# Second layer's mixture of experts: fixed slots for the first two pairs, 2 MB weight loads in the loop, and rearranged scatters and tail work

## What is computed

```python
MOE_GROUPS, MOE_EXPERTS_PER_GROUP, MOE_TOP_K, MOE_HIDDEN = 4, 8, 2, 512     # 32 experts
# router: one group of the four, then two of its eight experts; weights sum to the group's probability
# for every token: sum over its two experts of
#     weight * (silu(x @ w_gate[e]) * (x @ w_up[e])) @ w_down[e]
# w_gate, w_up: (32, 1024, 512)   w_down: (32, 512, 1024)
# then  h + expert sum, and a final rms_norm with gain final_norm_g
```

## Time and profile before

| | |
|---|---|
| median of 3 runs | 998.7 us (997.88 to 1004.07) |
| the profiled execution: span from the first to the last instruction | 997.7 us |
| bytes read from HBM | 338.07 MB |
| TensorE busy, weight loads of TensorE busy | 92%, 49% |
| VectorE, ScalarE, GpSimd busy | 30%, 21%, 2% |
| mean granted TensorE clock | 0.992 |

### The profile page before, as it was taken

The page is one execution under the profiler, slowest core; times in us unless marked ns, Lnnn a source line. Parts: engine busy times, 40 slices in busy tenths (PEclk is TensorE's granted clock), DMA queues, the critical chain, the costliest instruction groups (busy, mean ns, idle before and its releaser), DMA issues.

```text
span 997.7 us, 11975 instructions
## 1 busy us (share of the span) xinstructions
PE 915.7 (92%) x4621; PEld 486.7 (49%) x4621; DVE 304.2 (30%) x658; ACT 207.9 (21%) x440; POOL 22.9 (2%) x60
## 2 busy tenths in 40 slices
PE   8998999999999998999999999988887788887996
PEld 5776566555655555866447333333333233333332
DVE  3345357333332334132126132222201122201113
ACT  3232353112111114024324111111101111101112
POOL 4001300000000000000000000000000000000000
PEclk9999999999999998999999999999999999999999
DMA  9940455999999999644228999999999999999994
GB/s 312 388 174 1 168 191 206 422 420 422 419 421 421 419 421 388 247 143 168 85 82 349 423 415 422 420 421 421 422 422 422 421 423 421 422 422 421 422 422 191
DMA packets 62607, 339.77 MB, mean 341 GB/s; under 512 B 10877, under 2 KB 11921, under 8 KB 25570
## 3 DMA queue, kind: packets, MB, share of 16 engines
q1 hardware_dynamic: 56690, 337.60, 83.8%
q10 hardware_dynamic: 5456, 1.39, 0.7%
q0 software_dynamic: 416, 0.16, 0.2%
HBM read 338.07 MB, written 1.05 MB: 340 GB/s over the span
## 4 chain that ended last, share of the span: by engine, by line
PE 63%; DMA 28%; DVE 5%; ACT 2%; issue 1%; SPq 0%; DVEq 0%; ACTq 0%
DMA ring<-in_expert_w_up_dram 23%; PE ps L1005 22%; PE ps L1069 9%; PE ps L2070 7%; PE ps L2218 5%; PE ps L2283 4%; PE ps L1088 4%; DMA ring<-in_expert_w_down_dram 2%; DMA ring<-in_w_up_dram 2%; PE ps L2058 1%; PE ps L967 1%; PE ps L1195 1%; PE ps L1382 1%; PE ps L2193 1%; PE ps L1017 1%
## 5 line engine op out<-in xcount | busy, mean ns | idle before, releaser
L1005 PE MATMUL ps<-ring,work 128*64 128x256 f32 (+1 forms) x2048 | 344.3, 489 | 48.0 <-DMA ring<-in_expert_w_up_dram 23.9
L1005 PEld LDWEIGHTS ps<-ring,work 128*64 128x64 f32 x2048 | 151.6, 137 | 242.0 <-issue 207.1
L1069 PE MATMUL ps<-ring,work 128*64 128x512 f32 x688 | 156.1, 598 | 1.1 <-DMA ring<-in_expert_w_down_dram 0.9
L823 DVE TENSOR_TENSOR work<-work,ps 128x256 f32<-128x256 f32 (+1 forms) x30 | 16.4, 546 | 275.8 <-PE ps L1005 275.8
L1069 PEld LDWEIGHTS ps<-ring,work 128*64 128x64 f32 x688 | 47.9, 136 | 88.7 <-issue 88.2
L2070 PE MATMUL ps<-xT,ring 128*128 128x256 f32 (+1 forms) x384 | 86.3, 383 | 0.0
L2070 PEld LDWEIGHTS ps<-xT,ring 128*128 128x128 f32 x384 | 72.5, 191 | 11.4 <-issue 1.2
L1088 PE MATMUL ps<-parts 128*128 128x512 f32 x248 | 73.5, 419 | 2.2 <-DVE parts L844 2.2
L676 ACT ACTIVATE work<-ps,small 128x512 f32<-128x512 f32 x30 | 20.6, 688 | 196.6 <-PE ps L1069 196.6
L670 ACT ACTIVATE work<-ps 128x256 f32<-128x256 f32 (+1 forms) x31 | 15.1, 489 | 212.4 <-PE ps L1043 212.4
L2218 PE MATMUL ps<-ring,work 128*128 128x512 f32 x128 | 56.0, 595 | 2.2 <-ACT work L1708 1.8
(11 more groups left out here) (380 smaller groups left out, 676.3 us busy)
## 6 DMA issues: line engine op xcount, KB each, us to landing
ring<-in_expert_w_gate_dram SPq DMA_DIRECT2D x64, 1024.0 KB, 23.4
ring<-in_expert_w_up_dram SPq DMA_DIRECT2D x64, 1024.0 KB, 23.6
ring<-in_expert_w_down_dram SPq DMA_DIRECT2D x58, 1024.0 KB, 22.8
ring<-in_w_gate_dram SPq DMA_DIRECT2D x32, 1024.0 KB, 16.8
ring<-in_w_up_dram SPq DMA_DIRECT2D x32, 1024.0 KB, 18.3
ring<-in_w_down_dram SPq DMA_DIRECT2D x32, 1024.0 KB, 15.9
ring<-in_w_in_dram SPq DMA_DIRECT2D x18, 1024.0 KB, 15.6
ring<-in_w_out_dram SPq DMA_DIRECT2D x8, 1024.0 KB, 11.4
```

The costliest lines, as they stand in the source:

```text
L823: dve.tensor_tensor(hs[:, 0:ff], sil[:, 0:ff], ps[:, 5, 0:ff], ALU.mult).then_inc(ev(f"h{sfx}"), 1)
L1005: mm = pe.matmul(ps[CAP * e:CAP * e + CAP, 4 + which, 0:ff], slots, chunks[e][:, k, :], start=(k0 + k == 0), stop=(k0 + k == KC - 1), skip ...
L1069: mm = pe.matmul(ps[CAP * e:CAP * e + CAP, 6 + half, :], hT[:, c0 + k, CAP * e:CAP * e + CAP], columns(chunks[e], k, half), start=(c0 + k ...
```

## The change

- **Fixed slots.** Experts 0 to 3 (pairs 0 and 1) get 64 fixed slots each. Their one-hot rows (`fixed`) need only each token's place within its expert, not the packed order. `gather_fixed` forms them with 32 matmuls of 256 columns; VectorE and ScalarE (`take_fixed`) copy the result straight to `xg2`, each feature block when it is done, and the gates of pair 0 start block by block. The packed gather is still made, for pairs 2 to 15: its 32 matmuls of 512 columns stand in `opening` in two parts (`gather_rest`), and `onehot` is written behind the fixed copies.
- **Order and asides.** `OPENING` streams gates and ups of pairs 0 and 1 first, then both downs. The 6 chunks beside the ring are others: one of pair 0's gates, one of its downs, all 4 of pair 2's downs. Five of their loads stand ahead of place 8 in SP's order (`load_aside_early`), the rest ahead of place 12. GpSimd copies a row of numbers for the one-hot rows, so that its old place can take weights.
- **2 MB loads.** For pairs 4 to 13 (the loop) one load brings a whole matrix of one expert into two neighbouring slots (`load_whole`), 16 KB in a row in each partition. It waits until both slots are free: 3 or 4 chunks of a group of four used. TensorE waits for both experts' matrices at once.
- **Spread scatters.** In the loop (`spaced_pair`) the first half of pair n-1's scatter stands ahead of pair n's gates, the second between gates and ups.
- **Tail.** The gain row is loaded by ScalarE's queue and spread in pair 12, the residual rows are added in pair 13, both between gates and ups; pairs 12 and 13 are written out for that. Some loads of the tail wait for one more used chunk.

```diff
+def whole_weights(gate, up, down, ff, pair):
+    out = []
+    for w, c, n in ((gate, KC, ff), (up, KC, ff), (down, ff // P, D)):
+        v = w[0].rearrange("e (p c) n -> e p c n", c=c)
+        for e in range(2):
+            out.append((v[bass.ds(2 * pair + e, 1), :, :, :].rearrange("e p c n -> p (e c) n"), (c, n)))
+    return out
...
-        ASIDE = {"m1": (0, 0, 0), "m2": (4, 0, 2)}
...
+        ASIDE = {"m1": {}, "m2": {(0, 3): "aside3", (0, 11): "aside_pieces1", (2, 8): "aside0", (2, 9): "aside2",
+                                  (2, 10): "aside1", (2, 11): "aside_pieces0"}}
...
+        OPENING = ([(0, j) for j in range(8)] + [(1, j) for j in range(8)] + [(0, j) for j in range(8, 12)]
+                   + [(1, j) for j in range(8, 12)])
...
+        def two_slots(slot, shape):
+            return ring[:, slot:slot + 2, :].rearrange("p s n -> p (s n)").rearrange("p (a b) -> p a b", b=shape[1])
+        WHOLE = {"m1": PAIRS, "m2": 4}
+        WHOLE_LAPS = LAST_A - WHOLE["m2"]
...
+            def load_whole(n0, spec, turn, per_turn, freed):
+                src, shape = spec
+                sp.wait_ge(chunk_used, turn * per_turn + (n0 - RING + freed))
+                sp.dma_start(two_slots(n0 % RING, shape), src).then_inc(landed[n0 % RING], 16)
...
+            def load_aside_early(cfg):
+                sp.wait_ge(ev("rs_ready"), 8)
+                load_whole_aside(cfg, "aside0")
                 for k in range(2):
                     for half in range(2):
...
+                        load_piece(cfg, "aside_pieces0", k, half)
+                sp.wait_ge(*nth("vdp", 2))
+                load_whole_aside(cfg, "aside2")
+                load_piece(cfg, "aside_pieces1", 1, 0)
+                sp.wait_ge(*nth("numbers", 1))
+                load_piece(cfg, "aside_pieces1", 0, 0)
+                sp.wait_ge(ev("mTp"), 4)
+                load_piece(cfg, "aside_pieces1", 1, 1)
+                load_whole_aside(cfg, "aside3")
+            def load_aside_late(cfg):
+                sp.wait_ge(ev("router_pe"), 3)
+                load_whole_aside(cfg, "aside1")
+                sp.wait_ge(ev("routed"), 2)
+                load_piece(cfg, "aside_pieces1", 0, 1)
...
+                            if tag == "m2" and place == cfg["base"] + RING - 4:
+                                load_aside_early(cfg)
+                            if tag == "m2" and place == cfg["base"] + RING:
+                                load_aside_late(cfg)
...
+                            if p0 >= WHOLE[tag]:
+                                wholes = whole_weights(cfg["gate"], cfg["up"], cfg["down"], cfg["ff"], i * 2 + (p0 + k))
+                                for w, spec in enumerate(wholes):
+                                    load_whole(place_in_stream(cfg, p0 + k, 2 * w), spec, i, 2 * cfg["per"], 3 - w % 2)
+                                continue
...
+                        if j < RING and j % 4 == 1:
+                            sp.wait_ge(chunk_used, cfg["tail"] + j - RING + 2)
                         load(cfg["tail"] + j, spec, 0, 0)
-                        if j == 0:
-                            sp.dma_start(gain_row[0:1, :], t["final_norm_g_2"].rearrange("(a n) -> a n", a=1))\
-                                .then_inc(ev("gain_row"), 16)
...
+            pool.wait_ge(ev("odp"), TT)
+            pool.tensor_copy(numbers, from_one[:, :]).then_inc(ev("numbers"), 1)
...
+            def take_fixed(f):
+                act.wait_ge(*nth("fixed_pe", f // 2 + 1))
+                act.activation(xg2[:, :, f, :], ps[:, f // 2, 256 * (f % 2):256 * (f % 2) + 256]
+                               .rearrange("p (b s) -> p b s", b=2), ACT.Copy, scale=gk[:, cfg["gains"], f:f + 1])\
+                    .then_inc(ev("fixed_scalar"), 1)
...
-                bring(1, 1, ev("xg"))
                 take_gates(0)
+                take_gathered(1)
                 take_turned_hidden(n)
-                bring(2, 0, ev("xg"))
+                take_gathered(3)
                 take_gates(1)
+                take_gathered(5)
+                take_gathered(7)
                 take_down(0)
                 take_turned_hidden(n + 1)
+                act.wait_ge(ev("placed"), 5 * TURN[tag])
+                act.wait_ge(ev("xgP_even"), 4 * TURN[tag])
+                act.wait_ge(ev("xgP_odd"), 4 * TURN[tag])
+                bring(2, 0, ev("xg"))
...
                 build_weighted(0, n)
                 hidden(n, 0)
+                take_gathered(0)
+                take_gathered(2)
+                hidden(n + 1, 1)
+                take_gathered(4)
+                take_gathered(6)
                 take_scatter(n)
                 build_weighted(1, n + 1)
...
+            def gather_fixed():
+                def slots_of(f, tt, v, first, last):
+                    return pe.matmul(ps[:, f // 2, 256 * (f % 2):256 * (f % 2) + 256], v[:, tt, f, :].bitcast(F32R),
+                                     fixed[:, tt, :].bitcast(F32R), start=first, stop=last, skip_group_check=True)
+                for tt in range(TT):
+                    pe.wait_ge(ev("xs_high"), TT * turn_ + tt + 1)
+                    pe.wait_ge(*nth("fixed", tt + 1))
+                    for f in range(KC):
+                        slots_of(f, tt, xs_high, tt == 0 and f % 2 == 0, False)
+                for tt in range(TT):
+                    pe.wait_ge(ev("xs_low"), TT * turn_ + tt + 1)
+                    for f in range(KC):
+                        mm = slots_of(f, tt, xs_low, False, tt == 1)
+                        if tt and f % 2:
+                            mm.then_inc(ev("fixed_pe"), 1)
+            def gather_rest(groups):
+                pe.wait_ge(ev("onehot"), TT * TURN[tag])
+                for f in groups:
+                    if f >= 4:
+                        pe.wait_ge(ev("xgP_odd" if f % 2 else "xgP_even"), 4 * turn_ + (f - 4) // 2 + 1)
+                    else:
+                        pe.wait_ge(*nth("fixed_scalar" if f % 2 else "fixed_vector", KC // 2))
+                    for tt in range(TT):
+                        part(f, tt, xs_high, tt == 0, False)
+                        mm = part(f, tt, xs_low, False, tt == 1)
+                    mm.then_inc(ev("gathered"), 1)
...
+                    if pair >= WHOLE[tag]:
+                        for e in range(2):
+                            first = place_in_stream(cfg, pair, j - j % 4 + 2 * e)
+                            if j % 4 == 0:
+                                pe.wait_ge(landed[first % RING], turn * (16 * (2 * per // RING)) + 16 * (first // RING + 1))
+                            views.append(chunk_view(first % RING + j % 4 // 2, shape))
+                        return views
...
-                j = gates_and_ups(getter(0, 0), chunk_used, n, 0, True)
+                j = gates_and_ups(getter(0, 0), chunk_used, n, 0, pair=0)
+                gather_rest((0, 1))
                 turn_hidden(n)
+                gather_rest((2, 3))
+                gates_and_ups(getter(1, 0), chunk_used, n + 1, 1, pair=1)
+                gather_rest((4, 6, 5, 7))
                 turn_weights(n)
-                gates_and_ups(getter(1, 0), chunk_used, n + 1, 1)
                 down(getter(0, 0), chunk_used, j, n, pair=0)
+                pe.wait_ge(ev("xgP_even"), 4 * TURN[tag])
                 scatter(n, 0, True, False)
                 turn_hidden(n + 1)
+                pe.wait_ge(ev("xgP_odd"), 4 * TURN[tag])
...
+            def spaced_pair(pair, p0, turn, n):
+                scatter(n - 1, 0, False, False)
+                def between():
+                    scatter(n - 1, 1, False, False)
+                    if isinstance(pair, int) and pair == LAST_A - 2:
+                        spread_gain_row()
+                    if isinstance(pair, int) and pair == LAST_A - 1:
+                        for half in range(2):
+                            add_rows(half)
+                j = gates_and_ups(getter(p0, turn), chunk_used, n, p0 % 2, between=between)
+                if isinstance(pair, int) and pair == LAST_A - 2:
+                    pe.wait_ge(*nth("gain_ready", 2))
+                turn_hidden(n)
+                turn_weights(n)
+                down(getter(p0, turn), chunk_used, j, n, pair=p0)
             if tag == "m2":
+                gather_fixed()
                 opening(EARLIER[tag])
+                two_pairs(1, 1, 0, False)
+                turns = (LAST_A - 4) // 2 - 1
+                with pe.Fori(0, turns) as i:
+                    for odd in range(2):
+                        spaced_pair(None, 4 + odd, i, i * 2 + (EARLIER[tag] + 4 + odd))
+                for odd in range(2):
+                    p = 4 + 2 * turns + odd
+                    spaced_pair(p, 4 + odd, turns, EARLIER[tag] + p)
...
+            row = {"m1": from_one[:, :], "m2": numbers}[tag]
+            if tag == "m2":
+                dve.wait_ge(*nth("numbers", 1))
```

(17 more changed lines are left out.)

244 lines of the change are left out of this document (132 added, 112 removed).

## The result

| | before | after |
|---|---|---|
| median of 20 runs each | 999.9 us | 995.8 us |
| lowest, highest | 997.9, 1006.5 | 994.5, 999.7 |
| ratio, 95% interval | | 0.995, 0.9932 to 0.9967 |
| profiled execution, span | 997.7 | 993.7 |
| last load landed on its last engine | 984.34 | 980.34 |

The change is worth 0.5%, 4 to 5 us, less than the 1% that the prediction takes for no change. The span is 4.0 us shorter, and the last load lands 4.0 us earlier; from there to the end it is 13.4 us in both.

What follows compares the result with a forecast made beforehand. From pair 4 on the weights' DMA rate (422 GB/s) was taken as the bound. Span 997.7 less 2.0 (opening) and 4.5 (2 MB loads), nothing for scatters and tail, gave 991.2, so 992.2 us for the median; range 988.5 to 1001.

Steps and rivals of the forecast that it cites:

- the 1% that the prediction takes for no change: Whole kernel: about 1% (10 us) is what a measurement can tell from no change.
- The call, within 1% and a little faster: Whole kernel: 992.2 us forecast; chance 0.80 of within 1%, 0.13 of faster by more, 0.07 of slower.
- The prediction's narrower range, 989 to 995: Whole kernel: the forecast's own range, from 0 to 3.6 us for the opening and 2.2 to 5.1 for the packets.
- Gates at 537.8, SP's place 12 at 541.5: Opening: second layer's first gates start at 537.8 instead of 542.7, 4.9 us earlier; SP issues place 12 at 541.5.
- TensorE spends the head start: Pairs 0 to 3: added TensorE work uses up the 4.9 us and loses 1.4; pair 3 starts at 614.7.
- The pause ahead of the first 2 MB load: Before pair 4: place 42 needs 33 used chunks, not 31, waits until 621.6; a DMA pause of over 3 us.
- The opening's term, 2.0: Opening: places 42 and 43 land at 629.4 instead of 631.5, 2.1 us gained, taken as 2.
- A constant lag of the last engine: Weight stream: the most backward DMA engine sets the time; the pause lets it catch up, later instruction fetches may undo that.
- The rate, 4.5 us: Loop: 16 KB packets cost 1.7% less than two of 8 KB, taken as 1.5% of 298 us, 4.5 us gained.
- Scatters and tail at nothing: Loop and tail: scatters lie under waits, moved gain and residual rows were hidden; gain nothing, bound 0.5 us.
- PEclk at 1.00 in the loop: Loop: sign that the forecast is right, TensorE's granted clock stays at 1.00.
- The slower rival: Loop: three waits a pair lower TensorE's clock, a pair takes 31.5 us, the kernel 1013.7; 5%.

Runs made afterwards that it cites:

- e1_small: The changed kernel with 1 MB loads in the loop instead of 2 MB loads; 997.4 us, ratio 0.9969 to before.
- e4_late_whole: The changed kernel with pairs 4 and 5 loaded in 1 MB chunks and 2 MB loads only from pair 6 on; 996.7 us, ratio 0.9968 to before.
- after_again: The changed kernel measured once more with nothing altered; 996.2 us, ratio 0.9953 to before.
- e2_split: The changed kernel with each 2 MB load of the loop issued as two of 1 MB, same waits; 1000.5 us, ratio 1.001 to before.
- e6_scatter_back: The changed kernel with both scatters of a pair back behind gates and ups in pairs 4 to 11; 995.6 us, ratio 0.9941 to before.
- e5_tail_back: The changed kernel with gain row and residual rows back in the tail, pairs 12 and 13 back in the loop; 998.5 us, ratio 0.9972 to before.
- e3_whole_only: The kernel before with only the 2 MB loads in its loop added; 998.4 us, ratio 0.9987 to before.
- e8_rows_early: e4_late_whole with the gain row made in pair 4 and residual rows added in pair 5 instead of 12 and 13; 994.7 us, ratio 0.9929 to before.
- e8_again: e8_rows_early measured once more, beside the changed kernel on one chip; 995.0 us, ratio 0.9933 to before.
- e3_again: e3_whole_only measured and profiled once more with nothing altered; 1004.5 us, span 1002.7.

## Why the prediction was right, and where its sum was not

The call, within 1% and a little faster, came true, and 995.8 lies in the range. The forecast was 992.2; the span came out at 993.7 where the sum had 991.2, so 2.5 us are missing. The other 1.1 us of the distance lie between span and median: the sum added 1.0, and the median of the kernel after is 2.1 above its profiled span. The prediction's narrower range, 989 to 995, is reckoned from the span of 997.7; from its own terms it is 990.0 to 996.5 for the median, so that 995.8 lies outside the one as written and inside the other. Point by point:

- **Gates at 537.8, SP's place 12 at 541.5.** 538.01 and 541.66. The narrow products took 3.83 us in the chain for 32 (4.08 as the record of the timeline), 0.12 to 0.13 each, as the lower bound said.
- **TensorE spends the head start.** Pair 2 at 591.1 and pair 3 at 614.7 were forecast; 591.79 and 615.33 came. Right, 0.6 to 0.7 us short.
- **The pause ahead of the first 2 MB load.** Forecast 621.6, measured 622.40, for the reason given (33 used chunks). e1_small and e4_late_whole show the reason: with 31 the rate falls to 328 and 348 GB/s for 2 us, and there is no such pause.
- **The opening's term, 2.0.** This is the first that failed. Landing of 42 and 43 was to be 629.4 and was 630.57 on the last engine; 631.5 for before was right to the digit (631.52). So the gain is 0.9 us, not 2.1: 0.8 us are lost by the later issue and 0.4 in the load itself (8.17 us to landing instead of 7.8). Even the 0.9 is the lag's: the mean of the 16 parts lands 0.9 us later than in before (629.75 against 628.84; after_again 629.74), because the pause costs more than the earlier start gives. In e2_split, with the same pause, place 43 landed at 631.14, and nothing was left at the end. The opening is worth 2.3 us of mean only where no pause follows (e1_small).
- **A constant lag of the last engine.** This is the second. In before the lag is 3.5 us at 614 and 3.5 at 984. In the kernel after the pause does what was forecast, it brings the lag down to 1.49; but it is 1.97 at 890.5 and 2.98 at 896.4, right behind a fetch packet of 1.07 us at 894.2, and 2.94 at the end. The 1.45 us are lost behind the opening. The prediction had named this (later instruction fetches delay one engine) and given it as a reason for 0; the sum took 2. Its size is partly luck: in after_again the last engine ends at 980.87, in the first profile at 980.34, with the same mean of the parts, 978.83.
- **The rate, 4.5 us.** From the first engine's landing of place 43 to that of the last load it is 352.90 us in before, 352.87 in e2_split and 348.32 in after: 4.6. By the mean of the parts it is 353.4, 353.6 and 349.1: 4.3. The term was right. The line through two packet sizes gave 610.8 ns for 16 KB, 1.7% less than two of 8 KB; 200 x 16 / (5886 - 656) is 612, 1.5% less, which is what the sum took after its discount. The Trainium skill, DMA: Bandwidth & Descriptors, section Measured, lists 425 GB/s for 16 MB, for loads issued from GpSimd, and asks for 1 MiB or more a load; the trace has 428 with 2 MB loads and 422 with 1 MB, for loads issued from SyncE, which is over 4 us on this kernel, so here the measurement decides.
- **Sum of the misses.** 1.17 at 42 and 43, 1.45 of lag: 2.6, against the 2.5 missing. So the opening's 2.0 was the term that failed, and nearly all of the change's time is the 2 MB loads': the mean end of the loads is 982.22 in before and 978.83 in after, 3.4 us, which is 4.3 from the packets less 0.9 from the opening and its pause.
- **Scatters and tail at nothing.** Right for the scatters (e6_scatter_back). For the rows of the tail the number did no harm, since the change moves them and the loads set the end, but the reason was wrong and its bound of 0.5 too narrow: without the move 2.6 us are lost (e5_tail_back). The reasoning was from before, where the second down waits; it was not asked whether it would still wait once the loads are 4 us earlier, though only 1.4 us were to spare there. In the kernel after it is 2.5 us, with 5.8 us of work gone.
- **PEclk at 1.00 in the loop.** It was 0.99; two groups took 8.8 us (the granted clock is 0.81 from 685 to 694, the first of them). The slower rival named the right mechanism and the right reason why it is hidden at first; the price it would have is seen in e5_tail_back, not in the loop but in the tail. The Trainium skill, TensorE: Matmul & The Clock Gate, Part 1, ties the fall to idleness: the trace agrees in that waits of 2.7 us are followed by slow groups more often than those near 1 us (19 of the 32 groups of 32 behind such waits in three profiles, 2 of all 27 in the kernel after), and shows slow groups also behind waits of 0.93 and 0.95 us.

## What to carry to other kernels

When the bound of a stretch is moved, work out anew how much the next engine has to spare up to the end: here before had 1.4 us, 4 us off the loads were more than that, and the same rows that cost nothing in before cost 2.6 in e5_tail_back. Larger loads free and claim their buffers in larger steps; put the first of them where the stream has slack (two pairs later here), not where a lead is just being handed over. A lead won ahead of a stream that never pauses counts only at its most backward DMA engine; to judge it, compare the mean of the 16 parts as well, which was the same to 0.01 us in the two profiles of the kernel after, where the last one differed by 0.5.

## What the runs showed of the hardware

- **A packet of 16 KB costs 612 ns where two of 8 KB cost 621**, by the share of the DMA engines' time in the loop (the 8 KB figure from the prediction's 310.6). That is 422 against 428 GB/s, and e2_split, which has the kernel after's waits and order but 8 KB rows in two loads for one, is back at 422.
- **An instruction fetch moves one DMA engine back by about 1.5 us, and it stays there.** The twelve profiles have 68 packets of 16 KB of the instruction queue between 632 and 970 us. Set the 16 landing times of a load just ahead of the packet beside those of the load four later: in 58 of the 68 cases one part has fallen back by 1.5 to 1.7 us and the other 15 keep their distances to 0.1 us. Without a packet between them, 665 of 720 such pairs of loads show no part moved by over 0.1 us, and the largest move, 0.93, is at a dip to 348 GB/s in e3_whole_only. The lag grows by 1 us or more only when the part was far back already, 7 times. It steps up by 1.0 to 1.7 us, 2.1 to 3.5 us behind a packet that takes 1.02 to 1.1 us, and holds until the queue pauses:

| kernel | fetch packet | step of the lag |
|---|---|---|
| after | 894.2 | 1.97 to 2.98 at 896.4 |
| after_again | 894.8 | 1.79 to 3.50 at 897.0 |
| e6_scatter_back | 895.5 | 1.81 to 3.18 at 897.7 |
| e1_small | 960.2 | 2.65 to 3.91 at 962.8 |
| e5_tail_back | 956.0 | 1.84 to 2.89 at 959.5 |
| e8_rows_early | 721.3 | 1.43 to 2.66 at 723.4 |
| e8_again | 967.2 | 2.27 to 3.64 at 969.8 |

  Most fetches fall on engines that are ahead: behind the one at 958.2 in before, the fifth of the 16 parts becomes the second to last, and the lag stays at 3.5. Why packets of 1.0 to 1.1 us cost 1.5, and which engine a fetch falls on, stays open, and no kernel was run that moves only a fetch. It follows that up to 1 us of the difference between two single profiles need not be the kernel's.
- **TensorE can wait 3.6 to 5.6 us at the start of the tail for nothing that the profile names.** It did in the profiles of e3_whole_only, e3_again and e4_late_whole, each time with a packet of the instruction queue 1.7 to 2.5 us ahead of the next product, and not in the others. That it waits for instructions is likely; what decides it stays open. A kernel with 1.4 us to spare in its tail, as before, would pay for most of such a wait; no profile of before shows one.
